# Sliding-window attention: probabilities normalised before they are turned, V as the stationary operand

## The reference

```
s = einsum('bqkgd,bckd->bkgqc', q_blk, k_blk) * ATTN_SCALE, masked to the band
m = maximum(max(s, -1), sink);  p = exp(s - m)
w = p / (sum(p, -1) + exp(sink - m))
o = einsum('bkgqc,bckd->bqkgd', w, v_blk);  mix = o @ w_o
```

## Time and profile before

| | us |
|---|---|
| median of 3 runs (2387.07 to 2387.99) | 2387.52 |
| span of the profiled execution | 2386.3 |
| TensorE busy | 2368.3 (99%) |
| VectorE busy | 1588.6 (67%) |
| ScalarE busy | 1140.5 (48%) |
| GpSimd busy | 40.1 (2%) |
| queue of the weight loads | 60.3% of 16 DMA engines' span |

### The profile page before, as it was taken

How to read it: one execution, slowest core, us unless ns; L and a number is a source line. 1 busy time by engine, 2 the same in 40 slices (tenths; PEclk the granted TensorE clock), 3 DMA queues, 4 the chain that set the end, 5 groups by cost and what they waited for, 6 DMA issues and landing times.

```text
span 2386.3 us, 32914 instructions
## 1 busy us (share of the span) xinstructions
PE 2368.3 (99%) x12818; PEld 2005.7 (84%) x12818; DVE 1588.6 (67%) x2171; ACT 1140.5 (48%) x1670; POOL 40.1 (2%) x85
## 2 busy tenths in 40 slices
PE   9999999999999999999999999999999999999998
PEld 8888888888888888888888888778888888888886
DVE  7888888885568556556556577876864654655655
ACT  5555555564355344445344354554543443443441
POOL 0000000000000000000000000000000000000000
PEclk9999999999999999999999999999999999999999
DMA  8766666656567666666666646336776666666663
GB/s 233 230 195 194 188 191 190 189 169 239 193 186 235 210 187 190 198 186 187 200 186 190 199 150 209 120 122 198 201 234 189 188 198 182 194 197 189 190 196 108
DMA packets 487828, 455.11 MB, mean 191 GB/s; under 512 B 13792, under 2 KB 360080, under 8 KB 485392
## 3 DMA queue, kind: packets, MB, share of 16 engines
q1 hardware_dynamic: 484608, 433.51, 60.3%
q0 software_dynamic: 3088, 19.79, 2.3%
HBM read 450.55 MB, written 2.16 MB: 190 GB/s over the span
## 4 chain that ended last, share of the span: by engine, by line
PE 93%; DVE 3%; DMA 2%; ACT 1%; issue 1%; SPq 0%; POOL 0%; DVEq 0%; ACTq 0%
PE ps L453 24%; PE ps L478 16%; PE ps L480 15%; PE ps L479 15%; PE ps L459 12%; PE ps L511 2%; PE ps L509 2%; PE ps L510 2%; PE ps L530 1%; DVE wlo L1270 1%; DMA raw<-in_a_w_in 1%; ACT whi L838 1%; PE ps L746 1%; PE ps L602 1%; PE ps L716 0%
## 5 line engine op out<-in xcount | busy, mean ns | idle before, releaser
L1270 DVE TENSOR_TENSOR wlo<-raw,whi 128x1024 fp32r<-128x1024 f32 x817 | 994.3, 1222 | 656.6 <-ACT whi L838 656.1
L838 ACT ACTIVATE whi<-raw 128x1024 fp32r<-128x1024 f32 x817 | 859.4, 1056 | 853.9 <-PE ps L480 461.2
L453 PE MATMUL ps<-actA,whi 128*128 128x512 f32 x2704 | 648.2, 392 | 0.8 <-DVE wlo L1270 0.5
L453 PEld LDWEIGHTS ps<-actA,whi 128*128 128x128 f32 x2704 | 497.2, 188 | 98.4 <-issue 0.7
L478 PE MATMUL ps<-whi,actB 128*128 128x512 f32 x1056 | 412.8, 391 | 0.1
L479 PE MATMUL ps<-wlo,actB 128*128 128x512 f32 x1056 | 411.1, 389 | 0.0
L480 PE MATMUL ps<-whi,actB 128*128 128x512 f32 x1056 | 411.1, 389 | 0.0
L459 PEld LDWEIGHTS ps<-actA,wlo 128*128 128x128 f32 x2704 | 347.2, 191 | 13.4
L459 PE MATMUL ps<-actA,wlo 128*128 128x256 f32 x2704 | 351.4, 283 | 0.0
L478 PEld LDWEIGHTS ps<-whi,actB 128*128 128x128 f32 x1056 | 198.3, 188 | 43.0 <-issue 1.3
L480 PEld LDWEIGHTS ps<-whi,actB 128*128 128x128 f32 x1056 | 198.3, 188 | 41.3
(11 more groups left out here) (215 smaller groups left out, 1674.3 us busy)
## 6 DMA issues: line engine op xcount, KB each, us to landing
raw<-in_mlp_w SPq DMA_DIRECT2D x512, 512.0 KB, 4.2
raw<-in_a_w_in SPq DMA_DIRECT2D x162, 512.0 KB, 4.4
raw<-in_a_w_out SPq DMA_DIRECT2D x64, 512.0 KB, 4.8
raw<-in_b_w_q SPq DMA_DIRECT2D x32, 512.0 KB, 5.2
raw<-in_b_w_o SPq DMA_DIRECT2D x32, 512.0 KB, 3.9
csb<-cs_rows POOLq DMA_DIRECT2D x8, 1024.0 KB, 6.7
raw<-in_kv_w SPq DMA_DIRECT2D x16, 512.0 KB, 3.8
gb<-in_ln_g POOLq DMA_DIRECT2D x4, 1024.0 KB, 7.3
```

What stands on the lines that cost most here:

```text
L453: e.matmul(ps[:, b, :], whi[:, s, k * P:(k + 1) * P], act[:, kt, :, :].rearrange("p a n -> p (a n)"), start=(kt == 0), stop=False)
L838: e.activation(whi[:, s, :], raw[:, r, :], ACT.Copy).then_inc(w_hi_done, C.up(w_hi_done))
L1270: e.tensor_tensor(wlo[:, s, :], raw[:, r, :], whi[:, s, :].bitcast(F32), ALU.subtract).then_inc(w_split, C.up(w_split))
```

## The change

- `output` and `otok` go, and so do o_transposes. `sums` now scales the probabilities: after the reciprocal, one VectorE multiplication of `pb`, 4 heads x 128 or 256 keys in place, by the reciprocal repeated along the keys, which counts the new semaphore `p_scaled`. `sums` of unit u+1 stands at the end of unit u.
- p_transposes waits for `p_scaled` and always works by 64-wide tiles (`by_halves` goes), and it waits for `o_split`.
- values: V (128x64) is the stationary operand and `pT` moves, 128 columns; the result is channel-major, two heads below each other, in bank 6. ScalarE and VectorE write its two parts straight into `actB`, 256 columns per unit, each unit counting `o_split`.
- On TensorE, scores(u+1) come first, then a chunk (with the query transposes in it in units 2, 6, 10), then the turning of unit u, then the other chunk, then values. Unit 14 has one chunk, all others two; there are 31 chunks in the units.
- On VectorE the rope halves move behind the copy of pT and behind the low part, and the two weight splits of those units behind the second half.

```diff
-FILLS_OF_UNIT = [2, 2, 2, 2, 2, 2, 2, 2, 2, 2, 2, 1, 1, 2, 2, 2]
-OUT_CHUNKS_IN_UNITS = 12
+FILLS_OF_UNIT = [2] * 14 + [1, 2]
+OUT_CHUNKS_IN_UNITS = 13
+OUT_AFTER_UNITS = [(1, 6), (0, 7), (1, 7)]
...
             def q_transposes(h):
-                if h == 0 and C.any(o_split):
+                if h and C.any(o_split):
...
+            def p_transposes(c):
+                e.wait_ge(p_scaled, C.next(p_scaled))
+                if C.any(o_split):
+                    e.wait_ge(o_split, C.now(o_split))
...
             def values(b, c, j):
...
-                for i in range(4):
+                emptied(6)
+                emptied(7)
+                C.n[o_split] += 1
+                for t in range(2):
                     for kc in range(1 + c):
                         for a in range(2):
-                            last = e.matmul(ps[a * HD:(a + 1) * HD, 6, i * HD:(i + 1) * HD],
-                                            pT[:, (1 + c) * i + kc, a * HD:(a + 1) * HD],
-                                            vtok[:, kc, kv * HD:(kv + 1) * HD], start=(kc == 0), stop=(kc == c))
+                            last = e.matmul(ps[a * HD:(a + 1) * HD, 6, t * P:(t + 1) * P],
+                                            vtok[:, kc, kv * HD:(kv + 1) * HD],
+                                            pT[:, (1 + c) * (2 * t + a) + kc, :], start=(kc == 0), stop=(kc == c))
...
-                e.wait_ge(o_split, 2 * (c // 2 + 1))
+                e.wait_ge(o_split, 4 * (c // 2) + 3 + c % 2)
...
 # TensorE
                 for u, (b, c, j) in enumerate(UNITS):
-                    p_transposes(c, j)
                     if u + 1 < len(UNITS):
                         scores(*UNITS[u + 1])
-                    filler()
-                    if u and UNITS[u - 1][2]:
-                        o_transposes()
+                    turn = (c, j) == (1, 0) and b < QB - 1
+                    filler({1: lambda: q_transposes(0), 2: lambda: q_transposes(1)} if turn else {})
+                    p_transposes(c)
+                    for k in range(FILLS_OF_UNIT[u] - 1):
+                        filler()
                     values(b, c, j)
...
 # ScalarE
                 for u, (b, c, j) in enumerate(UNITS):
-                    pT_out(c, j)
                     step()
...
                     if (c, j) == (1, 0) and b < QB - 1:
                         qT_out(0)
                         qT_out(1)
+                    pT_out(c)
+                    if u + 1 < len(UNITS):
+                        exps(UNITS[u + 1][1])
                     for k in range(FILLS_OF_UNIT[u] - 1):
                         step()
+                    o_hi(b, c, j)
...
 # VectorE
+                e.wait_ge(dve_step, C.now(dve_step))
+                w = T if c else P
+                e.tensor_tensor(pb[:, :, 0:w], pb[:, :, 0:w], rinv.unsqueeze(2).broadcast_to([P, 4, w]),
+                                ALU.mult).then_inc(p_scaled, C.up(p_scaled))
...
+                sums(UNITS[0][1])
                 for u, (b, c, j) in enumerate(UNITS):
                     if u + 1 < len(UNITS):
                         maxima(*UNITS[u + 1])
+                    turn = (c, j) == (0, 1) and b < QB - 1
+                    if not turn:
                         next_step()
...
+                    pT_out(c)
+                    if turn:
+                        q_rope(2 * ((b + 1) % 2), used[b + 1], (0,))
+                    for k in range(FILLS_OF_UNIT[u] - 1):
+                        if not turn:
+                            next_step()
+                    if u + 1 < len(UNITS):
+                        sums(UNITS[u + 1][1])
+                    o_lo(b, c, j)
+                    if turn:
+                        q_rope(2 * ((b + 1) % 2), used[b + 1], (1,))
+                        for k in range(FILLS_OF_UNIT[u]):
+                            next_step()
...
 # GpSimd
-            e.wait_ge(o_split, C.next(o_split, 2 * QB))
+            e.wait_ge(o_split, C.next(o_split, 4 * QB))
```

More of the change, by code:

```diff
@@ L405, in _ @@
                         load(w, r * 2 * P, nb * BLK, BLK)
-            rest = [("o", nb, c) for nb in (0, 1) for c in (6, 7)] + [("o", nb, c) for nb in (2, 3) for c in range(8)]
+            rest = [("o", nb, c) for nb, c in OUT_AFTER_UNITS] + [("o", nb, c) for nb in (2, 3) for c in range(8)]
             for kind, nb, r in FILLS[2:] + rest:
@@ L719, in scores @@
                         last.then_inc(full[bank], C.up(full[bank]))
[L721 to L736, removed]
+            def p_transposes(c):
+                e.wait_ge(p_scaled, C.next(p_scaled))
+                if C.any(o_split):
+                    e.wait_ge(o_split, C.now(o_split))
+                fill(6)
+                fill(7)
+                for k in range(4 * (1 + c)):
+                    head, at = (k // 2, k % 2 * P) if c else (k, 0)
+                    for a in range(2):
+                        tk = slice(a * HD, (a + 1) * HD)
+                        last = e.transpose(ps[:, 6 + a, k * HD:(k + 1) * HD], pb[tk, head, at:at + P], ident[tk, tk])
+                        if k == 4 * (1 + c) - 1:
+                            last.then_inc(full[6 + a], C.up(full[6 + a]))
@@ L749, in values @@
                 last.then_inc(full[6], C.up(full[6]))
[L751 to L754, removed]
             def project(nb, c):
@@ L767, in out_chunk @@
                     fill(b0 + 1)
[L768 to L772, removed]
-                    e.wait_ge(o_split, 2 * (c // 2 + 1))
-                    column_chunk_products(b0, actB, c, inside=inside)
+                e.wait_ge(o_split, 4 * (c // 2) + 3 + c % 2)
+                column_chunk_products(b0, actB, c, inside=inside)
             def attention():
@@ L817, in _ @@
             attention()
-            for nb in range(2):
-                for c in (6, 7):
-                    out_chunk(nb, c)
+            for nb, c in OUT_AFTER_UNITS:
+                out_chunk(nb, c)
             column_block(0, actB)
@@ L1887, in pT_out, with o_lo @@
                     free[7], C.up(free[7]))
-            def o_lo(u):
-                b, c, _ = UNITS[u]
-                e.wait_ge(full[7], C.next(full[7]))
-                lo(actB[:, 4 * b:4 * b + 4, 1, c * P:(c + 1) * P], tiles(7),
-                   actB[:, 4 * b:4 * b + 4, 0, c * P:(c + 1) * P], o_split)
+            def o_lo(b, c, j):
+                kt, tk = 2 * (2 * b + j), slice(c * P, (c + 1) * P)
+                lo(actB[:, kt:kt + 2, 1, tk], ps[:, 6, 0:T].rearrange("p (t n) -> p t n", n=P),
+                   actB[:, kt:kt + 2, 0, tk], o_split)
             def attention(used):
@@ L1929, in attention @@
                         C.n[full[7]] += 1
+                    pT_out(c)
+                    C.n[full[6]] += 2
+                    if turn:
+                        q_rope(2 * ((b + 1) % 2), used[b + 1], (0,))
                     for k in range(FILLS_OF_UNIT[u] - 1):
-                        next_step()
-                        if u == len(UNITS) - 1 and k == 0:
-                            o_lo(u)
+                        if not turn:
[7 more added lines that the diff above has]
+                            next_step()
             for i in range(2, 8):
```

75 lines of the change are left out of this document (14 added, 61 removed).

## The result

| | before | after |
|---|---|---|
| median of 10 runs (lowest to highest) | 2387.95 (2387.07 to 2389.46) | 2394.61 (2392.06 to 2397.04) |
| span of the profiled execution | 2386.3 | 2392.8 |

The profiled execution after took 2394.57 us. The ratio is 1.0027, 95% interval 1.0019 to 1.0035: the kernel became 6.7 us slower, 0.28%. The forecast was 2391.5, 4.0 over the median shown then, 0.17%. The time lies in the range, the sign is right and the size is 2.7 us short, and it falls past the 0.2% that I called distinguishable (the interval begins just under it), where I had put 0.42 against 0.48 for "within".

What follows compares the result with a forecast made beforehand. TensorE, busy 99%, bounds the kernel now; after the change VectorE's chain would lengthen turn periods. The stretch sums to 3 x 35.05 + 31.6 = 136.8 against 132.9, +3.9 us, so about 2391.5, range 2383.5 to 2398.

Steps and rivals of the forecast that it cites:

- The loop: Each of three turn periods, through VectorE's and ScalarE's work and then TensorE's: 35.05 us against 33.90, +1.15.
- the walk: Attention stretch summed piece by piece in engine order: three periods of 35.05 plus 31.6, 136.8 us against 132.9.
- the values: TensorE's value products, half as many instructions of twice the columns: 0.95 and 0.52 us, gain 0.44 per period.
- TensorE alone: TensorE's own work in a period of four attention units, without waits: some 0.9 us less, 33.0.
- the switch from values to scores: On TensorE, values running straight into scores: loss between 0 and 0.09 us, taken as 0.06, four per period.
- the last period: Last four attention units, no rope: 31.6 us, with values in unit 14 waiting some 3 us for the copy.
- my interpolation from the scores: Cost of TensorE's new values taken from the scores' 1.01 us, between bounds 0.86 and 1.72: 0.95 and 0.52.
- the scaling: VectorE's normalisation of the probabilities, in a turn period's chain at 0.61 and 1.14 us.
- B: Rival: TensorE stays the bound, rope and scaling hide on VectorE; stretch 128.6 us, time 2383.2; chance 0.20.
- C: Rival: TensorE's column halves do not overlap at 128 columns, values take 1.72 us; time 2397.7; chance 0.12.
- D: Rival: VectorE's scaling with a zero-step repeated factor runs at half pace, +7.0 us; time 2398.5; chance 0.10.
- A: The forecast itself for the whole kernel: 2391.5 us, own range 2389.5 to 2394; chance 0.50.

Runs made afterwards that it cites:

- e12: Changed kernel with VectorE's late pT copies directly behind the maxima, ScalarE's rounding before exponentials except units 1, 5, 9, unit 14's turning before its chunk: 2385.49 us, ratio 0.9990.
- e7: Changed kernel without the scaling of the probabilities, a 4-column operation in its place: 2391.51 us, ratio 1.0012 to the kernel before.
- e11: Changed kernel with VectorE's copy of pT directly behind the maxima in units 2, 6, 10, 14 and all splits behind it: 2387.89 us, ratio 0.9999.
- e2: Changed kernel with ScalarE copying both halves of pT in unit 14 alone: 2391.64 us, ratio 1.0013 to the kernel before.
- e4: Changed kernel with ScalarE's second rounding of a unit ahead of the next unit's exponentials: 2394.19 us, ratio 1.0022 to the kernel before.
- e6: Changed kernel with the scaling of the probabilities made twice: 2407.74 us, ratio 1.0081 to the kernel before.
- e10: Changed kernel, ScalarE copying both pT halves in units 2, 6, 10, 14, put-off splits behind the next maxima, unit 14's turning before its chunk: 2388.14 us, ratio 0.9997.
- e1: Changed kernel with ScalarE copying both halves of pT in units 2, 6 and 10: 2394.11 us, ratio 1.0025 to the kernel before.
- e8: Changed kernel, ScalarE copying both pT halves in units 2, 6, 10, and two splits of units 1, 5, 9 behind the next maxima: 2389.65 us, ratio 1.0004.

## Why the prediction was right or wrong

**Right: where and how long.** TensorE waits at each place that was named and at no other of any size: before values in units 2, 6, 10 ("about 1.5", 1.46), before it at the query transposes (0.28 and up to 0.7 on the weight loads), in unit 14 ("some 3", 3.14), each released by VectorE's copy of `pT` or the rope. The loop was walked at 35.05 and measured 35.21, and it is right piece by piece. From the turning of unit 4 to VectorE's next maxima it took 5.84 (1521.03 to 1526.87; the walk had 5.77), from there to the following maxima 11.70 (to 1538.57; 11.72), to the values 4.83 (1543.40; 4.84), and from there to the turning of unit 8 12.85 (1556.25; 12.72). So 0.13 of the 0.16 that a period is short lies in TensorE's own piece, which holds two of the values. The scaling's forms cost 1.2 and 0.7 as sized from the splits.

**Nearly right: TensorE alone.** 33.0 was forecast. In e12 the period is 33.64, and all that is left of waiting in it is that the second query transposes start 0.45 behind the product ahead of them (1533.06 to 1533.51), where the first ones start 0.23 behind: 33.4. The turning measured 0.64 as forecast, the switch from values to scores 0.05 (0.06). Of the 0.4 that is missing, the values are 0.28 (two of each size, 0.07 each).

**Wrong size: the values.** Forecast 0.95 and 0.52, measured 1.02 and 0.59: the new form saves 0.06 and 0.02, not 0.13 and 0.09. This is not hidden behind VectorE: the loop holds two values a period and the last period two more, so the error is 8 x 0.07, nearly 0.6 us of the stretch. The Trainium skill, TensorEngine Tiling (Array Packing), Instruction Overhead, by which 64 columns already pay their way and halving the instructions saves nothing, was a little nearer: its 1.08 and 0.61 are 0.06 and 0.02 above the measured times, my interpolation from the scores 0.07 below both.

**The failed step: the last period.** "Unit 14 ... values come straight after the turning and wait some 3 us for the copy. Then 0.95 + 2.95 + ..." The wait was right and what follows was priced at full speed. The term left out is the clock behind it: values 1.77 in place of 1.02, four products 1.86 in place of the 1.03 that such a start of a chunk takes (1545.07 to 1546.10: the first 0.33 and three of 0.23), together 1.6 us. The Trainium skill, TensorE: Matmul & The Clock Gate, What's actually happening, describes this: the clock is granted by how busy TensorE has lately been. The trace fits it: the granted clock was 0.54 in the 3.7 us behind the wait of 3.14 and 1.00 behind each of those of 1.46. Measured and forecast stretch differ by 139.1 - 136.8 = 2.3: 1.6 of clock, 0.5 of the three periods and 0.2 in the rest, and the last two are for the most part the values. The time rose by 6.7 and not 4.0, so 2.3 of the missing 2.7 us are in this stretch, and the clock is most of it.

**Wrong reading: what the loop is made of.** I wrote the scaling into the loop at its full 0.61 and 1.14, as if there were no other way around it. e7 shows a second path of nearly the same length (values of unit 1, high part, low part, rope, splits), so taking the two scalings of a turn away gains 0.36 and not 1.75. The part common to both paths is what matters: rope half, two splits, maxima, a third split, all ahead of the copy. I noted that the two late splits are needed six chunks later, and didn't ask what they are ahead of.

**Rivals.** B's time (2383.2) did not come, as forecast, because the order on VectorE is fixed; but its mechanism is real, since e11 and e12 get within 0.7 us of its period (33.71 and 33.64 against 33.0) by reordering. C is refuted: 16 instructions take 1.02 and not 1.72, so the column halves overlap. D is refuted: 1225 ns for 128x1024 and not 2.4 us.

**The chances.** A at +0.17% was put at 0.30 within and 0.20 above the bound. What the walk left at nothing, the state of the clock behind a 3 us stop, could only add; the split should have leaned to the slower side.

## What to carry to other kernels

Where each engine works through a queue in a fixed order, look at what stands ahead of the instruction that the critical engine waits for: work with slack (here weight splits that TensorE needs six chunks later) goes behind it. Ten splits moved behind four copies in VectorE's queue were worth 6.7 us, all that the change had lost, while taking away the added instruction itself was worth some 3. Price an instruction on each path that ends at the same wait and not on the longest alone, and price a stop of TensorE like those of 2 to 4 us here with its clock as well, some 1.5 us.

## What the runs showed of the hardware

The clock behind a single stop of TensorE in this stretch. It stayed at 2.4 GHz behind idle times of 1.26 (e2), 1.46 (`after`), 1.84 (e4), 1.91 (e7), 2.26 and 2.43 us (e6), and fell to 1.2 behind 2.03 (e11), 2.11 (e10), 2.44 (e6), 3.14 (`after`), 3.15 (e1, e8) and 3.93 (e6). Windows of e11, e6 and e4 behind such a stop:

```profile
1605.76:1609.50 3.74, 3.74 (x22) 2.95 (x23) 3.25 (x6) 2.71 (x9) 0.00 (x0) 0.58 0.32 110
```

```profile
1541.50:1545.20 3.70, 3.70 (x16) 2.66 (x18) 3.67 (x4) 0.60 (x1) 0.00 (x0) 0.54 0.30 89
```

```profile
1611.20:1615.00 3.80, 3.74 (x28) 3.06 (x28) 2.94 (x5) 2.10 (x7) 0.00 (x0) 1.00 0.43 142
```

What a fall costs is read from the restart to the end of the next chunk. Values and chunk take 3.97 us at 2.4 GHz (1.02 + 2.95); behind the stop in unit 14 they took 5.54 in `after`, 5.36 in e1, 5.52 in e8 and 5.55 in e11. Turning and chunk take 3.59 (0.64 + 2.95), and took 5.19 in e10. That is 1.4 to 1.6 us lost each time. The fall need not be there at the restart: in e8 the values still took 1.10, and in e10 the turning (from 1603.34) its usual 0.64. TensorE's timeline of e10:

```profile
1604.32 0.40 PE L477 MATMUL ps<-wlo,actB 128*128 128x512 f32 x1
...
1604.92 0.63 PE L476 MATMUL ps<-whi,actB 128*128 128x512 f32 x1
```

Products came at full speed up to 1604.32, 1.0 us behind the restart, and every 0.43 us in place of 0.23 from 1604.92 on. Between 2.0 and 2.45 us the length of the stop alone doesn't decide, and what does was not settled. The spread of the times from run to run (5.0 us in `after`, 2.4 in the kernel before) is not explained by this: e2 kept its clock in unit 14 and spreads over 5.0 us too, and the kernel before spread over 4.5 in the 33 runs beside e7 to e10. The other surprise was the values: one new product of 128 columns takes 0.064 us (1.02 for 16) and two old ones of 64 columns took 0.068 (1.08 for 32), so there was hardly anything in the old form to remove.
